# Mixer early output units multiplied in float32 from the landed weights, gates moved ahead of the last taps

## The reference

```python
p = rms_norm(x) @ w_in            # 1024 -> a 256 | u 384 | v 384 | cv 384 | cg 384
ya = pool_mixer(a)                # trailing means of 2, 4, 8, 16 minus a, 64x64 products, scale
yb = u * (W_s norm(v) + b)        # gmlp: 4 heads of 96 features, blocks of 128 tokens
h  = cv * sigmoid(cg)
h  = depthwise_conv(h, 31 taps) + b
yc = silu(layer_norm(h)) @ w_pw + b_pw
x  = x + concat(ya, yb, yc) @ w_out
```

## Time and profile before

| | |
|---|---|
| median of 3 runs | 1728.29 us (1727.86 to 1729.78) |
| profiled execution, its own time | 1729.74 us |
| its span | 1727.8 us |
| PE busy | 1675.0 us (97%), 9952 matmuls |
| DVE busy | 1400.9 us (81%) |
| ACT busy | 1140.1 us (66%) |
| POOL busy | 247.9 us (14%) |

### The profile page before, as it was taken

The page is one execution under the profiler, slowest core; times in us unless marked ns, Lnnn a source line. Parts: engine busy times, 40 slices in busy tenths (PEclk is TensorE's granted clock), DMA queues, the critical chain, the costliest instruction groups (busy, mean ns, idle before and its releaser), DMA issues.

```text
span 1727.8 us, 26903 instructions
## 1 busy us (share of the span) xinstructions
PE 1675.0 (97%) x9952; PEld 1471.3 (85%) x9952; DVE 1400.9 (81%) x1570; ACT 1140.1 (66%) x1261; POOL 247.9 (14%) x251
## 2 busy tenths in 40 slices
PE   8999999998999999899999999999999999999998
PEld 8898898887899999788888888888888888888886
DVE  7667666769866658868898898898988998988897
ACT  5564555466654446577777777777777777777775
POOL 2212021148300004500010010010100100100100
PEclk9999999999999999899999999999999999999999
DMA  8333433243475464359999999999999999999994
GB/s 308 122 111 101 144 131 126 86 172 136 148 253 185 138 221 137 137 195 380 379 368 373 387 378 373 379 378 376 365 399 379 372 377 388 377 375 376 388 416 169
DMA packets 71046, 475.36 MB, mean 275 GB/s; under 512 B 8373, under 2 KB 9045, under 8 KB 19125
## 3 DMA queue, kind: packets, MB, share of 16 engines
q1 hardware_dynamic: 67205, 460.63, 70.7%
q0 software_dynamic: 3472, 12.60, 1.9%
q10 hardware_dynamic: 288, 1.05, 0.2%
HBM read 466.38 MB, written 7.86 MB: 274 GB/s over the span
## 4 chain that ended last, share of the span: by engine, by line
PE 79%; DVE 7%; issue 6%; ACT 4%; POOL 3%; DMA 0%; DVEq 0%; SPq 0%; POOLq 0%; ACTq 0%
PE bank L457 25%; PE bank L459 24%; PE bank L458 24%; DVE wlo L448 2%; ACT whi L443 2%; PE bank L1138 1%; POOL cacc L2402 1%; POOL pr L2312 1%; DVE bank L1895 1%; PE bank L760 0%; PE bank L1110 0%; PE bank L701 0%; POOL py L2384 0%; DVE sm L1776 0%; DVE rstd L1627 0%
## 5 line engine op out<-in xcount | busy, mean ns | idle before, releaser
L448 DVE TENSOR_TENSOR wlo<-raw,whi 128x2048 fp32r<-128x2048 f32 (+3 forms) x447 | 996.3, 2239 | 168.2 <-ACT whi L443 167.6
L443 ACT ACTIVATE whi<-raw 128x2048 fp32r<-128x2048 f32 (+3 forms) x447 | 833.4, 1865 | 220.4 <-PE bank L459 214.0
L457 PE MATMUL bank<-whi,hthi 128*128 128x512 f32 x896 | 354.2, 395 | 2.2 <-DVE htlo L2196 2.2
L459 PE MATMUL bank<-whi,htlo 128*128 128x512 f32 x896 | 350.3, 391 | 0.0
L458 PE MATMUL bank<-wlo,hthi 128*128 128x512 f32 x896 | 349.6, 390 | 0.0
L457 PE MATMUL bank<-uhi,whi 128*128 128x256 f32 (+2 forms) x1072 | 313.8, 293 | 6.5 <-DVE wlo L448 6.1
L459 PE MATMUL bank<-uhi,wlo 128*128 128x256 f32 (+2 forms) x1072 | 304.8, 284 | 0.0
L458 PE MATMUL bank<-ulo,whi 128*128 128x256 f32 (+2 forms) x1072 | 304.4, 284 | 0.0
L457 PEld LDWEIGHTS bank<-uhi,whi 128*128 128x128 f32 (+1 forms) x1072 | 201.8, 188 | 10.9 <-DVE wlo L448 7.9
L458 PEld LDWEIGHTS bank<-ulo,whi 128*128 128x128 f32 (+1 forms) x1072 | 201.9, 188 | 0.6
L459 PEld LDWEIGHTS bank<-uhi,wlo 128*128 128x128 f32 (+1 forms) x1072 | 201.6, 188 | 0.0
(11 more groups left out here) (366 smaller groups left out, 2100.9 us busy)
## 6 DMA issues: line engine op xcount, KB each, us to landing
raw<-in_wm SPq DMA_DIRECT2D x336, 1024.0 KB, 7.1
raw<-in_w SPq DMA_DIRECT2D x68, 1024.0 KB, 4.9
raw<-in_w SPq DMA_DIRECT2D x20, 768.0 KB, 4.3
raw<-in_w SPq DMA_DIRECT2D x16, 704.0 KB, 4.1
raw<-in_w SPq DMA_DIRECT2D x6, 512.0 KB, 3.7
y_slots<-zero POOLq DMA_DIRECT2D x4, 512.0 KB, 8.9
ys<-y_slots SPq DMA_DIRECT2D x4, 512.0 KB, 6.0
raw<-in_w SPq DMA_DIRECT2D x2, 576.0 KB, 3.9
```

The lines of the kernel that those rows point to most:

```text
L443: act.activation(whi[:, n % RING, 0:c], raw[:, n % RAW, 0:c], ACT.Copy).then_inc(hi_ready, 1)
L448: dve.tensor_tensor(wlo[:, n % RING, 0:c], raw[:, n % RAW, 0:c], whi[:, n % RING, 0:c].bitcast(F32), ALU.subtract).then_inc(lo_ready, 1)
L457: pe.matmul(out, s_hi, m_hi, start=start, stop=False, skip_group_check=shared)
L459: return pe.matmul(out, s_lo, m_hi, start=False, stop=stop, skip_group_check=shared)
```

## The change

- Early units 8, 9, 10 and 12 are no longer split. PE waits for their landing and multiplies them in one float32 matmul per part, straight from `raw`, with the moving side in float32 too: the gates from `gz`, the pooled parts from a new tile `pooled_out`. 48 products of three passes per mixer become 48 float32 matmuls.
- ScalarE and VectorE lose those four splits, the four mhi and four mlo instructions of pooled tiles and gates; ScalarE writes the two `pooled_out` tiles, in front of the products 25 to 30 instead of behind them.
- On VectorE both `take_pair` and the first gate stand ahead of the seven taps of the last unit, the second gate behind them.
- PE takes the gates' parts of unit 8 first, by pair, then the pooled parts.
- A `raw` slot of an early unit is free for the next load only at its `unit_done`. All counts of `hi_ready` and `lo_ready` skip the four units (`rounded`), and SP waits for the last early unit of the second mixer ahead of the expert loop.
- The reciprocal of `fin` moves behind the normalising products. The six moved taps of tile 2 stay as they were.

```diff
+FIRST_PART = POOL_T
+EARLY_PARTS = tuple(range(POOL_T, GM_T)) + tuple(range(POOL_T))
...
+WHOLE_UNITS = [base + u for base in UNIT_MIX for u in EARLY_UNITS]
...
+def rounded(n, per=0):
+
+    return n + 1 - sum(u <= n + (RAW if per else 0) for u in WHOLE_UNITS)
...
-            if n >= RAW:
-                sp.wait_ge(lo_ready, turn * per + (n - RAW + 1))
+            if n - RAW in WHOLE_UNITS and not per:
+                sp.wait_ge(unit_done, n - RAW + 1)
+            elif n >= RAW:
+                sp.wait_ge(lo_ready, turn * per + rounded(n - RAW, per))
...
+            sp.wait_ge(unit_done, WHOLE_UNITS[-1] + 1)
...
+                def early_unit(a):
+
+                    n = UNIT_MIX[L] + EARLY_UNITS[a]
+                    pe.wait_ge(raw_landed[n % RAW], 16 * (n // RAW + 1))
+
+                def early_parts(a, place, parts):
+
+                    n, d = UNIT_MIX[L] + EARLY_UNITS[a], 2 * a + place
+                    whole = raw[:, n % RAW, 0:unit_columns(n)].rearrange("p (k c) -> p k c", k=2 * GM_T)
                     for i in parts:
+                        rows = slice(0, P if i < POOL_T else GM_DIM)
+                        mix = pooled_out[:, i, :] if i < POOL_T else gz[0:GM_DIM, i - POOL_T, :]
+                        mm = pe.matmul(out_at(d), whole[rows, place * GM_T + i, :], mix, start=i == FIRST_PART and place == 0, stop=False,
+                                       skip_group_check=True)
                     return mm
...
+                early_unit(0)
                 pe.wait_ge(taken, TAKES * (L + 1))
+                for pair in range(2):
+                    pe.wait_ge(gm_ready, 2 * L + pair + 1)
+                    for place in range(2):
+                        early_parts(0, place, EARLY_PARTS[2 * pair:2 * pair + 2])
+                pe.wait_ge(mix_made, MIX_MADE * L + POOL_T)
                 for place in range(2):
+                    mm = early_parts(0, place, EARLY_PARTS[GM_HEADS:])
                 mm.then_inc(unit_done, 1)
+                mean()
                 early_unit(1)
-                early_tile(1, 0)
-                for c in range(CONV_T):
-                    pe.wait_ge(csq_ready, CONV_T * L + c + 1)
-                    mm = pe.matmul(bank[6][:, 0:SEQ], mean_c[:], csq[:, c, :], start=(c == 0), stop=(c == CONV_T - 1))
-                mm.then_inc(var_done, 1)
-                early_tile(1, 1).then_inc(unit_done, 1)
+                early_parts(1, 0, EARLY_PARTS)
+                variance()
+                early_parts(1, 1, EARLY_PARTS).then_inc(unit_done, 1)
                 early_unit(2)
-                early_tile(2, 0)
-                early_tile(2, 1).then_inc(unit_done, 1)
+                early_parts(2, 0, EARLY_PARTS)
+                early_parts(2, 1, EARLY_PARTS).then_inc(unit_done, 1)
                 early_unit(3)
-                early_tile(3, 0)
+                early_parts(3, 0, EARLY_PARTS)
...
-                for u in (GU_U, GU_U + 1):
-                    unit(u)
-                split_hi(act, n0 + EARLY_U + 2)
+                unit(GU_U)
                 act.wait_ge(par2_landed, 16 * PAR2)
                 for c in range(POOL_T):
-                    part(pool_done, L + 1, mhi[:, c, :], pool_out(c), ACT.Copy, scale=pools[:, L, c:c + 1])
-                for pair in range(2):
-                    hs = slice(2 * pair, 2 * pair + 2)
-                    part(gm_ready, 2 * L + pair + 1, mhi[0:GM_DIM, POOL_T + 2 * pair:POOL_T + 2 * pair + 2, :], gz[0:GM_DIM, hs, :], ACT.Copy)
+                    part(pool_done, L + 1, pooled_out[:, c, :], pool_out(c), ACT.Copy, scale=pools[:, L, c:c + 1])
+                unit(GU_U + 1)
...
-                        take_pair(0)
+                        for pair in range(2):
+                            dve.wait_ge(unit_done, n0 + GU_U + pair + 1)
+                            take_pair(pair)
+                        gate(0)
...
+                        gate(1)
+
                 conv_taps(L, done, len(taps))
                 conv_sums(L)
...
-                split_lo(dve, n0 + EARLY_U + 2)
 
                 dve.wait_ge(mean_done, L + 1)
...
                 split_lo(dve, n0 + PW_U)
-                if L == 0:
-                    dve.reciprocal(fin[:], fin[:]).then_inc(frs_ready, 1)
                 dve.wait_ge(csd_ready, L + 1)
                 dve.reciprocal(crs[:, 1, :], crs[:, 0, :]).then_inc(crs_ready, 1)
                 dve.wait_ge(crs_ready, L + 1)
                 for c in range(CONV_T):
                     dve.tensor_tensor(cacc[:, c, :], cacc[:, c, :], crs[:, 1, :], ALU.mult).then_inc(cn_ready, 1)
-                split_lo(dve, n0 + PW_U + 1)
+                if L == 0:
+                    dve.reciprocal(fin[:], fin[:]).then_inc(frs_ready, 1)
                 for c in range(CONV_T):
                     dve.wait_ge(chi_ready, CONV_T * L + c + 1)
                     dve.tensor_tensor(clo[:, c, :], csq[:, c, :], chi[:, c, :].bitcast(F32), ALU.subtract).then_inc(clo_ready, 1)
                 split_lo(dve, n0 + LATE_U)
```

More of the change, by code:

```diff
@@ L313, in build_program @@
         gvj = gz[:].rearrange("p h t -> p (h t)")[:, 0:2 * GM_HEADS * GM_DIM].rearrange("p (a c) -> p a c", a=2)
-        mhi = sb("mhi", [P, MIX_T, SEQ], F32R, scope=mixer)
-        mlo = sb("mlo", [P, MIX_T, SEQ], F32R, scope=mixer)
+        pooled_out = sb("pooled_out", [P, POOL_T, SEQ], scope=mixer)
+        mhi = sb("mhi", [P, CONV_T, SEQ], F32R, scope=mixer)
+        mlo = sb("mlo", [P, CONV_T, SEQ], F32R, scope=mixer)
         mixer.close()
@@ L920, in mixer_parts @@
                 mm.then_inc(pool_done, 1)
[L922 to L933, removed]
@@ new lines, in late_tile, with mean @@
+                def late_tile(n, d, place):
+                    hi, lo = unit_views(n, 4 * CONV_T)
+                    for f in range(CONV_T):
+                        at = place * CONV_T + f
+                        mm = three_pass(pe, out_at(d), hi[:, at, :], lo[:, at, :], mhi[:, f, :], mlo[:, f, :], False, f == CONV_T - 1, shared=True)
+                    return mm
+                def mean():
+                    pe.wait_ge(sum0_done, (L + 1) * PRODUCT_SUMS)
+                    pe.wait_ge(conv_ready, CONV_SUMS * (L + 1))
+                    for c in range(CONV_T):
+                        mm = pe.matmul(bank[5][:, 0:SEQ], mean_c[:], cacc[:, c, :], start=(c == 0), stop=(c == CONV_T - 1))
+                    mm.then_inc(mean_done, 1)
@@ new lines, in variance @@
+                def variance():
+                    for c in range(CONV_T):
+                        pe.wait_ge(csq_ready, CONV_T * L + c + 1)
+                        mm = pe.matmul(bank[6][:, 0:SEQ], mean_c[:], csq[:, c, :], start=(c == 0), stop=(c == CONV_T - 1))
+                    mm.then_inc(var_done, 1)
+                early_unit(0)
+                pe.wait_ge(taken, TAKES * (L + 1))
+                for pair in range(2):
+                    pe.wait_ge(gm_ready, 2 * L + pair + 1)
+                    for place in range(2):
+                        early_parts(0, place, EARLY_PARTS[2 * pair:2 * pair + 2])
@@ L1431, in unit @@
                     if u:
-                        split_hi(act, n0 + u + 2)
+                        if u + 2 not in EARLY_UNITS:
+                            split_hi(act, n0 + u + 2)
                         products(u)
@@ L1939, in mixer @@
                 for u in range(8):
-                    if u:
+                    if u and u + 2 not in EARLY_UNITS:
                         split_lo(dve, n0 + u + 2)
@@ L2018, in mixer @@
                 split_lo(dve, n0 + LATE_U)
-                hi_there(POOL_T + 2 + 1)
                 for f in range(CONV_T):
-                    hi_there(POOL_T + 2 + f)
-                    dve.scalar_tensor_tensor(mlo[:, GM_T + f, :], pw_out(f), convp[:, L, 3, f:f + 1],
-                                             mhi[:, GM_T + f, :].bitcast(F32), ALU.add, ALU.subtract).then_inc(mlo_ready, 1)
+                    dve.wait_ge(mix_made, MIX_MADE * L + POOL_T + max(f, 1) + 1)
+                    dve.scalar_tensor_tensor(mlo[:, f, :], pw_out(f), convp[:, L, 3, f:f + 1],
+                                             mhi[:, f, :].bitcast(F32), ALU.add, ALU.subtract).then_inc(mlo_ready, 1)
                 split_lo(dve, n0 + LATE_U + 1)
```

78 lines of the change are left out of this document (26 added, 52 removed).

## The result

The changed kernel took 1733.18 us (median of 18 runs, 1731.17 to 1735.94) beside 1728.51 us for the kernel before (18 runs, 1725.36 to 1730.38): ratio 1.0029, 95% interval 1.0022 to 1.0036, so 5.0 us slower with about 1.2 us to either side. The prediction was 1730.4 us in a range of 1725.0 to 1735.0. The time lies inside and on the side that the sum gave, but 0.29% is more than the 0.2% that the text called "within".

What follows compares the result with a forecast made beforehand. PE bounds the kernel (79% of the chain of waits). After V (variance end) -0.2 and +1.95, V itself -0.1 and +0.3, weights 0: +1.95, taken as +2.1 us on the median 1728.29, so 1730.4 us, range 1725.0 to 1735.0.

Steps and rivals of the forecast that it cites:

- within: Whole kernel: a difference up to about 0.2%, 3.5 us, which a measurement can't tell from no change; chance 0.67.
- The float32 price: PE's early units: each float32 product costs 0.43 us instead of 0.357; after V (variance end), -0.2 and +1.95 us in the mixers.
- VectorE's cover: After V (variance end): VectorE's work, less 1.7 us, done by V + 9.2; pointwise unit at V + 10.2, cover at least 1 us.
- POOL's chain and the mean: Ahead of the mean: POOL resumes 1.4 us earlier, but ScalarE's new wait absorbs that; mean at 433.8 and 717.2.
- Rival (3): VectorE's takes and gates beside POOL's chain hold it up, +5.4 us in all: 1735.8 us; chance 0.06.
- Rival (4): ScalarE's new wait doesn't bind, products are ahead of it; all 2.7 us earlier per mixer: 1725.0 us; chance 0.05.
- The gap and the clock: PE idles 6.0 us ahead of the mean; the clock drops, and a 5.0 us low stretch costs half its length.
- Rival (1): The clock doesn't drop in the gap ahead of the mean; both low stretches go, -5.0 us: 1725.4 us; chance 0.10.
- Rival (2): The clock returns late, low for 7.7 us over mean and unit 9; +1.35 us per mixer, 1733.1 us; chance 0.13.
- from the late units on PE is continuous into the next stage, so the late start moves the end one to one: Behind the early units in each mixer: any shift of the late units' start shifts the end by the same amount.
- Part 3: Weight loads, some later as early units' raw slots free later: covered by PE's 8 us of late-unit work, cost 0.

Runs made afterwards that it cites:

- Experiment 4: Changed kernel without the six float32 products of the first tile of unit 12 per mixer, output not the reference's: 1729.37 us, one run.
- experiment 2: Changed kernel with ScalarE's two pooled copies behind products 25 to 30 instead of ahead of them: 1721.70 us, ratio 0.9958 to the kernel before.
- experiments 9 and 10: Result-row loads issued three weight loads later (ROWS_AT 15 instead of 12): 9 in the kernel before, 1728.06 us; 10 in the changed kernel, 1731.92 us.

## Why the prediction was right in its mechanism and short in its size

**The float32 price: right.** 24 products, between 441.25 and 451.44, take 10.19 us, 0.425 each, for the 0.43 taken from the earlier trace rows. After V it was to be 15.95 us, and is 15.93 in both mixers; against the earlier trace rows -0.2 and +1.9 us, for -0.2 and +1.95. Experiment 4 adds that PE alone counts there in mixer 2.

**VectorE's cover: clo isn't last, as forecast, but the removed split buys less of it than the text counted.** clo ends at 449.63, V + 8.2, and the pointwise unit starts at V + 10.0; the bound was V + 9.2, and less the 1.7 us of the split it would be V + 7.5. DVE, mixer 1, of the kernel before:

```profile
440.65 1.75 DVE L2008 RECIPROCAL fin<-fin 128x256 f32<-128x256 f32 x1
442.31 1.75 DVE L2010 RECIPROCAL crs<-crs 128x256 f32<-128x256 f32 x1
444.10 4.17 DVE L2013 TENSOR_TENSOR cacc<-cacc,crs 128x256 f32<-128x256 f32 x3
```

and of the changed kernel:

```profile
443.75 1.09 DVE L2023 TENSOR_TENSOR cacc<-cacc,crs 128x256 f32<-128x256 f32 x3
444.76 1.75 DVE L2025 RECIPROCAL fin<-fin 128x256 f32<-128x256 f32 x1
446.42 3.21 DVE L2028 TENSOR_TENSOR clo<-csq,chi 128x256 fp32r<-128x256 f32 x3
```

POOL's scaling now meets clo instead of the normalising, as the text had it, and costs less there: the two take 1.09 + 3.21 = 4.3 us for 4.17 + 1.08 = 5.25. What uses up the split's 1.7 us is the reciprocal of `fin`. The prediction counted it among the work behind V in both kernels; before, it stood at 440.65, ahead of V, where VectorE had the deviation to wait for, and now its 1.75 us stand between the normalising and clo. -0.95 - 1.75 + 1.75 us is the step from V + 9.2 to V + 8.2. In mixer 2 POOL has nothing beside clo (changed kernel):

```profile
729.67 1.10 DVE L2028 TENSOR_TENSOR clo<-csq,chi 128x256 fp32r<-128x256 f32 x3 [1.28 <-ACT chi L1513]
```

**POOL's chain and the mean: right to 0.4 us.** POOL was to resume at 416.3, and did at 415.62; the 25th product was to be added from 423.8, and was from 423.46; the mean was to start at 433.8 and 717.2, and did at 433.43 and 717.20. Counted from the start of the pooling matmuls, which takes out the early start of this execution, it was 12.5 us in both mixers for 12.3 in the sum. Rival (3) falls: no add takes over 0.8 us. Rival (4) falls as a forecast of this kernel, and is what experiment 2 makes of it: there the products are ahead of the copies. Its time was given as 1725.0, and 1721.7 came out: the shorter gap also spares the low clock in mixer 2 and part of it in mixer 1, which the rival's sum left in.

**The gap and the clock: right.** Idle 6.07 us for 6.0, low for 5.2 and 4.7 us behind the restart for 5.0. Rival (1) falls: the drop came later than 2.5 us after the stop, at 4.4 and 3.9, but still well inside the gap. Rival (2) falls too, though its 1733.1 is the time that was measured: the clock was back before the 6.4 us from which it was to decide.

**What was off, first: small terms up to the late units of mixer 2, 0.8 us in all.** The two mixers gave +2.8 us for the 1.95 to 2.1 of the sum. Against 1.95 it is 0.4 us in mixer 1 (+0.1 for a gain of 0.3): the 0.2 us of the chain up to the mean, and 0.1 for the low stretch of 5.2 us. It is 0.1 in mixer 2. The other 0.3 lie between: the sum had the pooling matmuls of mixer 2 0.3 us earlier against the late units of mixer 1, since the removed split frees the wait for gv. It does shorten the step from unit 7 to the pooling matmuls, by 0.26 us in mixer 1 (4.60 to 4.34) and 0.18 in mixer 2 (4.53 to 4.35). But ahead of unit 7 of mixer 2 the next stage takes 0.2 us more (242.99 instead of 242.80 from the late units of mixer 1, most of it by 471), so from late units to pooling matmuls it is 247.33 us before and 247.34 after.

**Second: "from the late units on PE is continuous into the next stage, so the late start moves the end one to one".** This holds up to the end of the units, and through the middle experts (119.1 us each). It failed in the routing, by 0.45 us in the first two pairs of profiles and 2.6 in the third, where the clock decides and the cause stays open, and in the last expert, by some 1.2 us (experiments 9 and 10), at a place where the kernel before lost 0.3 us in one profile and nothing in the other. Part 3 costed the weights at 0 by looking at the loads behind the early units; PE's own rows of the last expert, with ScalarE's wait of 2.17 us for a landing beside them, were not read. Both errors have one sign. With them the local sum is 2.8 + 0.45 + 1.2 = 4.5 us, for 5.0 measured, with 1.2 us to either side; the 0.5 us between are not resolved, and are within what the clock changes from one profile to the next.

**The chances.** With a sum of +2.1 us and a border at 3.5, 1.4 us of small errors were enough to change the answer from "within" to "slower". They were given 0.24, mostly for mechanisms; plain additions and the stretches behind the mixers, which none of the rivals names, did it. That 1733.2 still lies in the range is in part luck: the room above the forecast was there for rival (2) and for a dearer float32 product, and neither came.

## What to carry to other kernels

When work is moved to fill a gap on the bounding engine, ask which wait then ends last and whether something ahead of it in an in-order queue has just been given a new one: one line moved on ScalarE was worth 10 us in the two mixers, twice what the whole change had moved. Filling work is taken from a later gap, so it has to be measured out: one tile moved up across the mean left gaps of 0.45 and 0.59 us, two tiles left 0 and 3.18 us and brought the low clock back, 7.1 us in all by the medians. And where an argument says "from here on one to one", look up the narrowest place behind that point, here the one expert in which a weight lands late. Two profiles that agree to 0.2 us can still share one state of the clock; a third one showed another.

## What the runs showed of the hardware

A float32 product of 256 columns costs 0.425 us at 2.4 GHz, 1.19 times three float32r passes of the same width (0.357). The Trainium skill, "FP8 and Floating Point Precision", section "TensorE Precision Notes", has true FP32 as four passes through the array. Four thirds of 0.357 would be 0.476 us, an estimate from that page, and the trace is 0.05 us below it; but counted in clocks the trace agrees with four passes. 0.425 us are 1020 clocks, 4.0 for each of the 256 columns, while a float32r matmul's 0.119 us are 286 clocks, 1.1 for each: it is the three separate passes that take more than one clock a column.

The contention of VectorE and GpSimd showed on VectorE's side: clo 3.21 us beside POOL's scaling and 1.10 alone. The Trainium skill, "SBUF — State Buffer", section "Who interferes with whom", says that a VectorE instruction with two SBUF inputs contends with a GpSimd one that reads SBUF; both read so here, and the trace agrees, with a factor of 2.9.

The granted clock also fell with no idle PE. In both profiles of the changed kernel it was 0.50 for 10.2 us from about 753, in the routing, whose matmuls are 2 to 128 columns wide; PE was recorded as busy for all of it. In the kernel before it stayed at 1.00 behind the same matmuls, until a gap of 2.24 us, in two profiles, and fell among them, with PE busy, in the third (experiment 9). What decides between the two was not tried.
